# Two-block transformer on one core: the end of the last product and the final norm by halves of the tokens

## The reference

```python
def rms_norm(x, gain):
    x32 = x.astype(F32)
    y = x32 * lax.rsqrt(jnp.mean(jnp.square(x32), axis=-1, keepdims=True) + EPS)
    return (y * gain.astype(F32)).astype(x.dtype)
...
        h = rms_norm(x, norm_mlp[l])
        x = x + jnp.square(jax.nn.relu(h @ w_up[l])) @ w_down[l]
    return rms_norm(x, norm_final)
```

## Time and profile before

| | |
|---|---|
| timed runs | 1314.02, 1319.74, 1322.57 us; median 1319.74 |
| profiled execution, its own time | 1313.61 us |
| its span, first to last instruction | 1311.8 us |
| mean granted TensorE clock | 0.992 of full speed |
| TensorE busy, matmuls | 1278.8 us, 97% of the span |
| TensorE busy, weight loads | 1061.3 us, 81% |
| DVE busy | 803.4 us, 61% |
| ACT busy | 636.4 us, 49% |
| GpSimd busy | 154.1 us, 12% |
| DMA moved | 118.19 MB, 90 GB/s over the span |

### The profile page before, as it was taken

The page is one execution under the profiler, slowest core; times in us unless marked ns, Lnnn a source line. Parts: engine busy times, 40 slices in busy tenths (PEclk is TensorE's granted clock), DMA queues, the critical chain, the costliest instruction groups (busy, mean ns, idle before and its releaser), DMA issues.

```text
span 1311.8 us, 16468 instructions
## 1 busy us (share of the span) xinstructions
PE 1278.8 (97%) x6038; PEld 1061.3 (81%) x6038; DVE 803.4 (61%) x1542; ACT 636.4 (49%) x1235; POOL 154.1 (12%) x142
## 2 busy tenths in 40 slices
PE   7999999999999999999999999999999999999996
PEld 7888888878888888888787777888888888888885
DVE  5778789685664556356788877578644343344344
ACT  6686667454434433233555655476543242332343
POOL 0012211000110001000002101022311030110110
PEclk9999999999999999999999999999999999999998
DMA  7311110423332333332333212432333323233321
GB/s 265 89 41 32 49 33 25 141 83 91 102 96 73 113 104 96 95 91 81 112 89 98 79 57 57 125 105 77 97 94 94 96 78 114 80 112 97 96 80 64
DMA packets 63583, 118.19 MB, mean 90 GB/s; under 512 B 7696, under 2 KB 10128, under 8 KB 63248
## 3 DMA queue, kind: packets, MB, share of 16 engines
q1 hardware_dynamic: 62352, 113.48, 29.5%
q10 hardware_dynamic: 1152, 3.67, 0.9%
HBM read 115.02 MB, written 2.10 MB: 89 GB/s over the span
## 4 chain that ended last, share of the span: by engine, by line
PE 84%; DVE 5%; issue 5%; ACT 4%; DMA 1%; POOL 0%; POOLq 0%; SPq 0%; ACTq 0%; DVEq 0%
PE bank L564 24%; PE bank L566 24%; PE bank L565 24%; PE bank L757 2%; PE bank L642 2%; PE bank L643 2%; PE bank L644 2%; PE bank L743 1%; PE bank L744 1%; ACT tmp L1611 1%; DVE wl L1828 1%; ACT wh L1193 1%; DVE pp L1999 0%; DMA praw<-in_pT 0%; DVE qs L1915 0%
## 5 line engine op out<-in xcount | busy, mean ns | idle before, releaser
L1828 DVE TENSOR_TENSOR wl<-raw,wh 128x512 fp32r<-128x512 f32 (+2 forms) x360 | 267.5, 754 | 333.9 <-ACT wh L1193 333.3
L1193 ACT ACTIVATE wh<-raw 128x512 fp32r<-128x512 f32 (+1 forms) x398 | 242.1, 619 | 287.8 <-PE bank L566 275.8
L564 PE MATMUL bank<-AH,wh 128*128 128x512 f32 x832 | 327.7, 394 | 0.9 <-DVE AL L1842 0.3
L566 PE MATMUL bank<-AH,wl 128*128 128x512 f32 x832 | 326.7, 393 | 0.0
L565 PE MATMUL bank<-AL,wh 128*128 128x512 f32 x832 | 325.3, 391 | 0.0
L564 PE MATMUL bank<-BH,wh 128*128 128x512 f32 x624 | 248.2, 398 | 0.0
L566 PE MATMUL bank<-BH,wl 128*128 128x512 f32 x624 | 245.5, 393 | 0.0
L565 PE MATMUL bank<-BL,wh 128*128 128x512 f32 x624 | 244.5, 392 | 0.0
L564 PEld LDWEIGHTS bank<-AH,wh 128*128 128x128 f32 x832 | 156.3, 188 | 36.6 <-issue 3.6
L565 PEld LDWEIGHTS bank<-AL,wh 128*128 128x128 f32 x832 | 156.3, 188 | 34.4 <-issue 0.2
L566 PEld LDWEIGHTS bank<-AH,wl 128*128 128x128 f32 x832 | 156.3, 188 | 34.0
(11 more groups left out here) (303 smaller groups left out, 1623.4 us busy)
## 6 DMA issues: line engine op xcount, KB each, us to landing
raw<-in_w_dn SPq DMA_DIRECT2D x104, 256.0 KB, 2.7
raw<-in_w_gu SPq DMA_DIRECT2D x88, 256.0 KB, 2.6
raw<-in_w_up SPq DMA_DIRECT2D x64, 256.0 KB, 2.6
raw<-in_w_nsa SPq DMA_DIRECT2D x16, 256.0 KB, 2.7
raw<-in_w_pg SPq DMA_DIRECT2D x16, 256.0 KB, 2.6
raw<-in_w_naq SPq DMA_DIRECT2D x16, 256.0 KB, 2.7
nbi<-in_na_bias ACTq DMA_DIRECT2D x8, 448.0 KB, 3.4
raw<-in_w_swa SPq DMA_DIRECT2D x10, 256.0 KB, 2.8
```

Source lines behind the costliest of these rows:

```text
L564: t.matmul(o, w, xh, start=start, stop=False, skip_group_check=skip)
L566: return t.matmul(o, wl, xh, start=False, stop=stop, skip_group_check=skip)
L1193: a.activation(W[i % NW].h[:, 0:n], RAW[i % NRAW][:, 0:n], ACT.Copy).then_inc(*s_wh.up(i))
L1828: v.tensor_tensor(w.l[:, 0:n], RAW[i % NRAW][:, 0:n], w.h[:, 0:n], ALU.subtract).then_inc(*s_wl.up(i))
```

## The change

Chunks 6 and 7 of the last product, the final norm and the output are done by halves of the tokens: half 0 is tokens 0 to 255, half 1 tokens 256 to 511. TensorE does chunk 6 half 0, chunk 7 half 0, chunk 6 half 1, the sums of half 0, chunk 7 half 1, then spreads half 0's factor twice, does the sums of half 1 and spreads its factor twice. Each part has 24 matmuls of 256 columns. The sums now take the running sum of chunks 0 to 5 and the squares of 6 and 7 one after the other (three sources, two blocks of tokens each). On DVE the norm of half 0 stands ahead of chunk 7's addition of half 1, and the norm of half 1 behind the six multiplications of half 0. ACT's root table is loaded ahead of chunk 6's first square. GpSimd multiplies four halves. Stores take several chunks of one half each, in rows of 1 KB where they had 2 KB; SyncE issues seven and ACT, behind its last copy, two.

The diff without the hunk that declares a second semaphore for the stores:

```diff
         def half(g):
             return slice(64 * g, 64 * g + 64)
+        def of_tokens(h):
+            return slice(256 * h, 256 * h + 256)
         ff = list(range(22))
         sq_keys = [("n0", c) for c in range(1, 8)] + [("y1", c) for c in range(1, 8)] + [("x1", c) for c in range(1, 8)]
...
             if name == "w_out_ret":
                 return ("xr", i), 1
             return ("wos", i), 1
+        def last_store(e, c, n, h):
+            def part(t):
+                return t[:, T * c:T * (c + n)].rearrange("p (c k) -> p c k", c=n)[:, :, of_tokens(h)]
+            for k in range(c, c + n):
+                e.wait_ge(s_gp.at(("out", k, h)) if k > 5 else s_dv.at(("out", k, h)))
+            by = s_out2 if h and c in (0, 4) else s_out
+            e.op.dma_start(part(out), part(X)).then_inc(*by.up(("out", c, h), by=16))
         def tensor(e):
...
                 for i in range(2):
                     keys = [("xd", gi, 4 * i + g) for g in range(4)]
                     if gi == 3 and i:
-                        for g in range(4):
+                        for g in range(2):
                             product("w_dn2", 56 + 2 * g, A, up_ready, range(8), 1, 4, [keys[g]])
                             bank.give(keys[g])
                         continue
                     product("w_dn2", 16 * gi + 8 * i, A, up_ready, range(8), 4, 1, keys)
                     for key in keys:
                         bank.give(key)
-            soon("x5")
-            soon_back("x5")
-            b, free = bank.take(("bk2", "x5"))
-            e.wait_ge(*free)
-            for i in range(4):
-                c = slice(P * i, P * i + P)
-                m = t.matmul(b[:, c], ones[:, :], tmp.ap(("x5", "d"))[:, c], start=True, stop=True)
-            m.then_inc(*s_st.up(("bk2", "x5")))
-            bank.give(("bk2", "x5"))
+            def last_part(c, h):
+                key, o = ("xd", 3, c, h), of_tokens(h)
+                b, free = bank.take(key)
+                e.wait_ge(*free)
+                for s in range(2):
+                    w, i = weights("w_dn2", 48 + 2 * c + s)
+                    for j in range(4):
+                        x, col = A[4 * s + j], P * j
+                        e.wait_ge(up_ready(4 * s + j))
+                        m = triple(b[:, 0:256], w.h[:, col:col + P], x.h[:, o], x.l[:, o], w.l[:, col:col + P], s + j == 0, s == 1 and j == 3)
+                    done = ([("o", key)] if s else []) + ([("p", i)] if h else [])
+                    if done:
+                        m.then_inc(*s_mm.up(*done))
+                bank.give(key)
+            def last_sums(h):
+                b, free = bank.take(("st", "x5", h))
+                e.wait_ge(*free, s_ad.at(("x5", 5)))
+                for n, src in enumerate((r2_bc, sqr.ap(("x5", 6)), sqr.ap(("x5", 7)))):
+                    if n:
+                        e.wait_ge(s_sq.at(("x5", 5 + n, h)))
+                    for i in range(2):
+                        c = P * (2 * h + i)
+                        m = t.matmul(b[:, 64 * i:64 * i + 64], src[:, c:c + P], ones[:, 0:64], start=n + i == 0, stop=n == 2 and i == 1,
+                                     skip_group_check=True)
+                m.then_inc(*s_st.up(("x5", h)))
+                bank.give(("st", "x5", h))
+            def last_back(name, h):
+                b, free = bank.take((name, h))
+                e.wait_ge(*free)
+                for i in range(2):
+                    e.wait_ge(s_rs.at(("x5", "diag", 2 * h + i)))
+                    c = P * (2 * h + i)
+                    m = t.matmul(b[:, P * i:P * i + P], ones[:, :], tmp.ap(("x5", "d"))[:, c:c + P], start=True, stop=True)
+                m.then_inc(*s_st.up((name, h)))
+                bank.give((name, h))
+            last_part(6, 0)
+            last_part(7, 0)
+            last_part(6, 1)
+            last_sums(0)
+            last_part(7, 1)
+            last_back("bk", 0)
+            last_back("bk2", 0)
+            last_sums(1)
+            last_back("bk", 1)
+            last_back("bk2", 1)
         def scalar(e):
...
                             if i:
                                 hi(WHERE["w_dn2", k0 + 2 * g + 1] + 4)
                             c = 4 * i + g
-                            if c == 7:
-                                root_table("x5")
+                            if c > 5:
+                                continue
                             square("x5", c, chunk(X, c), s_sv.at(("xd", 3, c)))
                             e.wait_ge(s_sq.at(("x5", c)))
                             a.activation(chunk(X, c), chunk(X, c), ACT.Copy, scale=g2fin[:, c:c + 1]).then_inc(*s_cp.up(("xg", c)))
                     behind("w_dn2", k0 + 7)
-            soon("x5")
-            e.wait_ge(s_st.at(("bk2", "x5")))
-            a.activation(r_bc[:, :], bank.ap(("bk2", "x5"))[:, :], ACT.Copy).then_inc(*s_cp.up(("r2", "x5")))
+            def last_square(c, h):
+                e.wait_ge(s_sv.at(("xd", 3, c, h)), *sqr.before(("x5", c)))
+                a.activation(sqr.ap(("x5", c))[:, of_tokens(h)], chunk(X, c)[:, of_tokens(h)], ACT.Square).then_inc(*s_sq.up(("x5", c, h)))
+            def last_gain(c, h):
+                x = chunk(X, c)[:, of_tokens(h)]
+                e.wait_ge(s_sq.at(("x5", c, h)))
+                a.activation(x, x, ACT.Copy, scale=g2fin[:, c:c + 1]).then_inc(*s_cp.up(("xg", c, h)))
+            def last_root(h):
+                b = bank.ap(("st", "x5", h))[:, 0:128].rearrange("p (b q) -> p b q", q=64)[:, :, 0]
+                e.wait_ge(s_st.at(("x5", h)))
+                a.activation(rv[:, 4 + 2 * h:6 + 2 * h], b, ACT.Sqrt, bias=eps, scale=1.0 / 1024).then_inc(*s_fn.up(("x5", "sqrt", h)))
+            def last_spread(h):
+                e.wait_ge(s_st.at(("bk2", h)))
+                a.activation(r_bc[:, of_tokens(h)], bank.ap(("bk2", h))[:, 0:256], ACT.Copy).then_inc(*s_cp.up(("r2", "x5", h)))
+            root_table("x5")
+            last_square(6, 0)
+            last_gain(6, 0)
+            last_square(7, 0)
+            last_gain(7, 0)
+            last_square(6, 1)
+            last_root(0)
+            last_gain(6, 1)
+            last_square(7, 1)
+            last_spread(0)
+            last_gain(7, 1)
+            last_root(1)
+            last_spread(1)
+            for c, n in ((0, 2), (4, 2)):
+                last_store(e, c, n, 1)
         def vector(e):
...
                         ahead("w_dn2", k0, 8)
                     for g in range(4):
                         c = 4 * i + g
+                        if gi == 3 and c > 5:
+                            continue
                         x_add(c, ("xd", gi, c), ("xd", gi, c), s_sv.at(("xo", c) if gi == 0 else ("xd", gi - 1, c)), s_sq.at(("x4", c)),
                               s_xl.at(("x4", c)))
                         if gi == 3 and i:
                             lo(WHERE["w_dn2", k0 + 2 * g + 1] + 4)
-                        if gi == 3 and c < 7:
+                        if gi == 3:
                             add_square("x5", c)
                     behind("w_dn2", k0 + 7)
-            soon("x5")
+            def last_add(c, h):
+                key, x = ("xd", 3, c, h), chunk(X, c)[:, of_tokens(h)]
+                e.wait_ge(s_mm.at(("o", key)), s_sv.at(("xd", 2, c)), s_sq.at(("x4", c)), s_xl.at(("x4", c)))
+                v.tensor_tensor(x, x, bank.ap(key)[:, 0:256], ALU.add).then_inc(*s_sv.up(key))
+                bank.read(key, (s_sv, key))
+            def last_norm(h):
+                b = bank.ap(("st", "x5", h))[:, 0:128].rearrange("p (b q) -> p b q", q=64)[:, :, 0]
+                k, r, y, d = ("x5", h), rv[:, 4 + 2 * h:6 + 2 * h], rv[:, 2 * h:2 * h + 2], tmp.ap(("x5", "d"))
+                e.wait_ge(s_fn.at(("x5", "sqrt", h)))
+                v.reciprocal(r, r).then_inc(*s_rs.up((k, 0)))
+                e.wait_ge(s_rs.at((k, 0)))
+                v.scalar_tensor_tensor(out=y, in0=b, scalar=1024 * EPS, in1=r, op0=ALU.add, op1=ALU.mult).then_inc(*s_rs.up((k, 1)))
+                bank.read(("st", "x5", h), (s_rs, (k, 1)))
+                e.wait_ge(s_rs.at((k, 1)))
+                v.scalar_tensor_tensor(out=y, in0=y, scalar=-0.5 / 1024, in1=r, op0=ALU.mult, op1=ALU.mult).then_inc(*s_rs.up((k, 2)))
+                e.wait_ge(s_rs.at((k, 2)))
+                o = rv_out[:, 2 * h:2 * h + 2]
+                v.scalar_tensor_tensor(out=o, in0=y, scalar=1.5, in1=r, op0=ALU.add, op1=ALU.mult).then_inc(*s_rs.up((k, 4)))
+                e.wait_ge(s_rs.at((k, 4)), *tmp.before(("x5", "d")), s_tab.at("tab"))
+                for i in (2 * h, 2 * h + 1):
+                    v.tensor_scalar(d[:, P * i:P * i + P], ident[:, :], rv_out[:, i:i + 1], None,
+                                    ALU.mult).then_inc(*s_rs.up(("x5", "diag", i)))
+            def last_out(c, h):
+                x = chunk(X, c)[:, of_tokens(h)]
```

(32 more changed lines are left out.)

## The result

Faster by 0.26%: the median of 20 runs is 1315.40 us (1310.13 to 1318.12) against 1318.65 us for 20 runs of the kernel before (1313.12 to 1322.57), and the ratio of the two is 0.9974 with a 95% interval of 0.9963 to 0.9985. That is 3.4 us of 1318.65 (2.0 to 4.9 by the interval). The prediction said 3.2 us and 1316.5.

The account below looks back on a forecast made before the run. TensorE's matmuls were taken to bound the kernel, with a chain of engine waits in the last 26.6 us. A 0.3 us later last-factor point against 3.5 less behind it gave 3.2 less: 1316.5 us, range 1309.5 to 1320.5.

Parts of the forecast that it names:

- Matmuls by halves: Chunks 6 and 7 on TensorE: 96 matmuls of 256 columns, 0.117 us apart, take 11.23 us, 0.25 more.
- Weights: Chunk 7's first part starts earlier, at 1288.06 instead of 1290.74; its weights are ready 0.7 us early, no cost.
- Sums ahead of the last part: Half 0's sums on TensorE before the fourth part take 1.3 us; the product ends 1.55 us later.
- First norm: Half 0's norm on DVE runs beside the fourth part: no cost, ready with 1.0 us to spare.
- After the product: Steps from 1297.78: second norm 1300.5, second factor 1302.84 at half clock, last multiplication 1304.9, end 1308.6.
- GpSimd's half: GpSimd's multiplication of half a chunk: 0.68 us taken, between bounds of 0.41 and 1.25.
- Stores: Output at the end: first half gone by about 1303.1; second, 1.05 MB at 380 GB/s, takes 2.76 us to 1307.7.
- Sum: The whole span's end moves from 1311.8 to 1308.6, 3.2 us less.
- By parts: Last-factor multiplications start 0.3 us later; the stretch behind is 3.5 less through half multiplications, half bytes, no store gap.
- second rival: Final stores do not shrink with their bytes: 1 KB rows make the second half take 5.5 us, gain 0.4; chance 0.08.
- load pace: Rival on TensorE's short matmuls: weight loads set 0.188 us spacing, result 3.6 us slower (1323.3); chance 0.05.
- the overlap does not come about: Rival after the product: late squares or slow first multiplications delay the second half; gain 1.8 us (1317.9); chance 0.12.

Follow-up runs that it names:

- split_only: The kernel before with only chunks 6 and 7 multiplied as 96 matmuls of 256 columns; tail (chunk 6's first matmul to span end) 26.84 us, 26.55 before.
- sums_late: The changed kernel with half 0's sums, root and norm moved behind the last part of the product; tail 24.77 us against 23.01.
- sums8: The changed kernel with chunk 6's square added on DVE, so that TensorE's sums take 8 rows instead of 12; tail 22.55 us.
- norm_only: The changed kernel with chunks 6 and 7 whole (512 columns), only additions, squares, norm, scaling and stores by halves; tail 26.92 us, 26.81 when repeated.
- rows_1k: The kernel before with its eight 256 KB stores as two chunks by half of the tokens, in rows of 1 KB; tail 26.86 us.
- norm_busy: norm_only with six unread matmuls of 512 columns on TensorE behind each half's sums; tail 24.78 us.
- before_busy: The kernel before with six unread matmuls behind the sums, in TensorE's 1.57 us wait for the diagonals; tail 25.11 us.
- sums8_split: sums8 with the second norm behind four of six multiplications, ACT's second root earlier, the first half's last store split; tail 22.34 us, ratio 0.9963 to the kernel before.

## Why the prediction was right or wrong

*What bounds the kernel.* Right: the change acts on the last 26.6 us only. The rest moved with the granted clock and by a few tenths at the start, and the prediction had not foreseen the clock as the main cause of the runs' spread. It also said that 13 us is what a measurement can tell from no change; 20 runs of each told 3.4 us from none.

*Matmuls by halves.* Right: 0.118 apart (0.117 said), a cost of 0.3 alone (split_only).

*Weights.* Right: TensorE starts the first part of chunk 7 at its slot, without a gap (72 starts in 8.48 us).

*Sums ahead of the last part.* Right: they took 1.25 (1.3 said). The product ended 12.64 into the tail (12.53 said).

*First norm.* Right: it is hidden, ready 1.1 before it is wanted (1.0 said).

*After the product.* The last addition came at 12.84 (12.73 said), the first multiplications at 13.29 (13.15 said) and the second norm at 15.31 (15.25 said), where it met the end of the six multiplications, as said. The second factor came at 17.26 where the sum had 17.62: here the low clock was taken and the full one granted, 0.36 better (the prediction had named 0.5 for it). The clock counted once more in the second spreading, so ACT's copy started 17.70 into the tail where the working had 18.4, and the second burst could begin the earlier. The reason given, "because TensorE idles here as it does now", failed: the wait is as long (1.55), but up to it TensorE had worked without a gap, where before it had idled 0.6 us a little earlier (1297.2 to 1297.84) and done only small matmuls. The length of the matmuls ahead of the waits is not what decides: split_only has 256 columns and the two waits of before, and its factor was spread at 0.50 (2.04 us), while sums_late has 256 columns, none of the 0.6, twice the 1.55, and stayed at 1.00. Nor is it the longer wait alone: sums8 stood idle for 1.95 us at a stretch ahead of its second factor and took 1.13 for it. In each execution whose clock fell TensorE had also been held up among the sums (0.60 us; in norm_only eight of their rows took 1.39 us for 1.06), in those of the changed kernel, sums_late and sums8 it had not. That this first hold-up has a part in the fall is not shown by an experiment.

*GpSimd's half.* It took 0.71 each (0.68 said). *Stores.* The first burst was done 18.5 into the tail (17.9 said). The second ran from about 19.0 to 22.1, over 3.1 us where 2.76 was said: this is the term that was undersized, by the 10% that rows of 1 KB cost (rows_1k). The second rival had this mechanism at a price that was far too high, and the estimate from the Trainium skill's "DMA: Bandwidth & Descriptors", section "Why small descriptors are slow (HBM only)", was 4.5%: the sign and half the size.

*Sum.* The prediction said 3.2; it is 3.54 in the tail and 3.4 timed. Two wrong terms partly cancel: the clock made ACT's copy, and with it the start of the second burst, 0.7 earlier, and the rows made that burst 0.34 longer. So part of the agreement is luck.

*By parts.* This is where the prediction was right for a reason that it had not seen. It put the gain down to "half the multiplications, 1.05 MB and not 2.1 to move, no gap between stores". As an account of two timetables that is true, as a cause it is not: norm_only has the half multiplications and the half bytes behind its last factor and is slower than the kernel before, and with its clock kept (norm_busy) it is still only 0.33 below before_busy. The experiments order the 3.54 as follows:

| step | tail, us | worth |
|---|---|---|
| before | 26.55 | |
| full clock kept through the norm (before_busy) | 25.11 | 1.44 |
| and additions, norm, scaling, stores by halves (norm_busy) | 24.78 | 0.33 |
| matmuls in halves instead of unread ones to keep the clock (sums_late) | 24.77 | 0.01 |
| first norm beside the last part (the change) | 23.01 | 1.76 |

Half of the gain is the first norm beside the second half's product, two fifths are the clock, and halving bytes and multiplications by itself gives a tenth: the chain of small steps has to be gone through twice, so the last factor comes at 19.00 in norm_busy and at 16.43 in before_busy, and that eats most of what the shorter stretch behind it gives (5.78 us for 8.68). The steps are not independent, and another order of them would share out the gain otherwise; without the clock, halves are a loss (norm_only, 26.92). Each tail but those of the change and of norm_only is from one execution. That the clock is a part of the change's own gain is shown by the rows (1.13 at 1.00 for 2.05 at 0.50); that its part is 1.44 is shown for the kernel before, and is inferred for the change.

*Rivals.* The load pace is refuted (split_only). Of the stores the mechanism was right, but the price is 0.3 instead of 2.8. That the overlap does not come about is refuted: it did come about, and the multiplications came every 0.33.

## What to carry to other kernels

A dependent chain at the end of a kernel is worth splitting where its first pass can run beside the last product; splitting a chain that runs after the product gave almost nothing here (0.33 us), as its small steps are paid twice. Look at the granted clock in such a chain: six matmuls that nobody reads, put in one of TensorE's waits, took 1.44 us off a tail of 26.55. And where the change is at one end of the program, compare a stretch that starts at a fixed instruction, not spans.

## What the runs showed of the hardware that was not expected

- The granted clock fell to 0.50 inside a tail in which TensorE had two short waits (0.6 and 1.57 us) between small matmuls, and did not fall when the longer one was filled (before_busy; in norm_busy both waits of 1.55). In the changed kernel the same wait of 1.55 us passed at 1.00. At 0.50 eight fp32 rows of 128 columns take 2.05 us, at 1.00 they take 1.13.
- Early in the program, 52 to 78 us, the granted clock was 1.00 in one profiled execution and 0.80 to 0.86 in the twelve others. Against the execution after the change that stretch is worth 4.8 us. It is not the only one: sums8_split had 0.80 there and yet reached chunk 6 at 1286.16, 0.91 behind the first, because it had 1.00 at 130 to 156, 260 to 286 and 754 to 780, where the first had 0.93 each time. This, not the change, is why the spans of the two profiled executions differ the wrong way.
- Stores with rows of 1 KB moved 334 to 350 GB/s in full slices, with rows of 2 KB 375 to 391. With rows of 1 KB it made no difference to the tail whether SyncE issued all of them (22.91) or SyncE and ACT (22.96 to 23.01).
